# Attention of one hybrid layer: reciprocals by a small transposing transfer, both first scores ahead of the values, output weights loaded over a longer time

## The reference, cut to what matters

```python
s  = jnp.einsum('bqhd,bkhd->bhqk', qi, k).astype(jnp.float32) * ATTN_SCALE
pr = jax.nn.softmax(s, axis=-1).astype(v.dtype)
return jnp.einsum('bhqk,bkhd->bqhd', pr, v)
```

```python
mixed = jnp.concatenate([out_a, out_b, out_c], axis=-1)
return jnp.einsum('bnm,md->bnd', mixed, P['w_out'][l]), ckv, k_rope
```

## Time and profile before

| | |
|---|---|
| time, three runs | 1521.13, 1522.87 (median), 1523.97 us |
| profiled execution | 1522.13 us, its span 1520.2 us |
| granted TensorE clock | 0.997 of full speed |
| busy share of the span | PE 97%, PEld 78%, DVE 40%, ACT 27%, POOL 18% |
| attention, groups 0 to 3 | 273.5 to 352.9, to 430.5, to 508.2, to 608.1 us |

### The profile page before, as it was taken

The page is one execution under the profiler, slowest core; times in us unless marked ns, Lnnn a source line. Parts: engine busy times, 40 slices in busy tenths (PEclk is TensorE's granted clock), DMA queues, the critical chain, the costliest instruction groups (busy, mean ns, idle before and its releaser), DMA issues.

```text
span 1520.2 us, 25562 instructions
## 1 busy us (share of the span) xinstructions
PE 1480.5 (97%) x10145; PEld 1180.3 (78%) x10145; DVE 605.1 (40%) x1385; ACT 408.0 (27%) x933; POOL 280.3 (18%) x308
## 2 busy tenths in 40 slices
PE   6999999999999999999999999999999999999997
PEld 3654545666666655444899999999999999999996
DVE  2211446676868673136683222222222222222215
ACT  2400102555646452235321111111111111111114
POOL 0005400463747463110000100100000000000000
PEclk9999999999999999999999999999999999999999
DMA  9971001475747593541587999999889989899885
GB/s 364 353 261 50 32 0 41 82 137 104 142 98 144 130 200 73 194 166 70 191 322 271 323 294 312 315 353 300 291 316 296 362 293 300 313 292 357 291 260 223
DMA packets 313917, 338.79 MB, mean 223 GB/s; under 512 B 209091, under 2 KB 210666, under 8 KB 311678
## 3 DMA queue, kind: packets, MB, share of 16 engines
q1 hardware_dynamic: 308814, 319.58, 66.4%
q0 software_dynamic: 4752, 17.30, 4.4%
q10 hardware_dynamic: 288, 1.05, 0.2%
HBM read 266.18 MB, written 21.64 MB: 189 GB/s over the span
## 4 chain that ended last, share of the span: by engine, by line
PE 88%; DVE 5%; DMA 4%; ACT 2%; issue 1%; POOL 0%; SPq 0%; DVEq 0%; ACTq 0%; POOLq 0%
PE ps L1286 32%; PE ps L1315 16%; PE ps L678 8%; PE ps L1016 7%; PE ps L915 6%; PE ps L969 4%; DMA wreg<-wreg 2%; PE ps L703 2%; PE ps L869 2%; PE ps L693 1%; PE ps L894 1%; PE ps L881 1%; DVE stat L1921 1%; PE ps L710 1%; DMA wreg<-x_rows 1%
## 5 line engine op out<-in xcount | busy, mean ns | idle before, releaser
L1286 PE MATMUL ps<-mreg,wreg 128*128 128x144 f32 x4096 | 506.3, 286 | 0.0
L1286 PEld LDWEIGHTS ps<-mreg,wreg 128*128 128x128 f32 x4096 | 503.4, 190 | 0.7 <-ACT hreg L1625 0.4
L1315 PE MATMUL ps<-mreg,wreg 128*128 128x144 f32 x2048 | 256.4, 286 | 2.1 <-DVE mreg L2365 2.1
L1315 PEld LDWEIGHTS ps<-mreg,wreg 128*128 128x128 f32 x2048 | 253.1, 190 | 2.5 <-DVE mreg L2365 2.3
L2365 DVE TENSOR_TENSOR mreg<-ps,mreg 128x144 f32<-128x144 f32 x128 | 39.4, 307 | 357.6 <-PE ps L1286 346.7
L2530 POOL COPY wreg<-hreg 128x1024 uint16<-128x1024 uint16 x128 | 146.2, 1168 | 156.7 <-ACT hreg L1504 156.1
L915 PE MATMUL ps<-wreg 128*128 128x512 f32 (+2 forms) x400 | 159.0, 520 | 3.8 <-ACT hreg L1504 3.7
L1662 ACT ACTIVATE mreg<-ps 128x144 f32<-128x144 f32 x128 | 37.2, 291 | 426.1 <-PE ps L1286 426.1
L1016 PE MATMUL ps<-wreg,mreg 128*128 128x512 f32 x288 | 130.5, 598 | 0.0
L678 PE MATMUL ps<-hreg,wreg 128*128 128x512 f32 (+1 forms) x400 | 128.9, 480 | 0.0
L2577 POOL DMA_INDIRECT x_rows<-hreg,idx_s x15 | 23.9, 1596 | 533.1 <-DVE hreg L2342 521.6
(11 more groups left out here) (310 smaller groups left out, 1217.7 us busy)
## 6 DMA issues: line engine op xcount, KB each, us to landing
wreg<-in_w_e_dram SPq DMA_DIRECT2D x96, 2048.0 KB, 12.4
wreg<-in_w_ada_dram SPq DMA_DIRECT2D x16, 1024.0 KB, 8.3
wreg<-in_w_ada_dram SPq DMA_DIRECT2D x16, 512.0 KB, 10.9
wreg<-in_w_out_dram SPq DMA_DIRECT2D x8, 512.0 KB, 4.2
wreg<-in_x_sample_dram SPq DMA_DIRECT2D x8, 512.0 KB, 4.6
x_rows<-wreg SPq DMA_DIRECT2D x8, 512.0 KB, 3.5
xn_rows<-wreg SPq DMA_DIRECT2D x8, 512.0 KB, 2.6
wreg<-x_rows SPq DMA_DIRECT2D x8, 512.0 KB, 8.5
```

Source lines behind the costliest of these rows:

```text
L1286: mm = pe.matmul(o[:, 0:CAP], w[s][:, k, (f % 4) * P:(f % 4 + 1) * P], xsT[b][:, k, :], start=(k == 0), stop=(k == KD - 1))
L1315: mm = pe.matmul(bank[4 + dm % 2][:, 0:CAP], w2[f // 4][:, f % 4, dm * P:(dm + 1) * P], hidT[:, f, :], start=(f == 0), stop=(f == 7))
```

## The change: what it does

1. The reciprocals are turned by a transfer. POOL writes them, spread to 64 columns and split into 16-bit halves, into `rest_halves` (128 x 256 halves for a pair); SP issues one transposing transfer for the pair behind the four others (`turn_rest`), and ACT joins the halves into a part of `probT` (`rest_joined`). The 36 matmuls with the unit matrix and ACT's 36 copies out of their bank are gone. POOL waits for the small transfer of the pair before (`rest_turned`) before it writes the reciprocals of an even n. The constant `EXTRA` is 0, so that nothing else goes by this way.
2. In ACT's order the join of the reciprocals stands between the two exponentials of a pair, and not before the first.
3. At the start of a group PE makes the scores of n = 0 and n = 1 and then all values. ACT copies the values out instead of DVE.
4. Of the eight parts of the output weights two are loaded in group 1 and two in group 2 (behind n = 5 and n = 9), and four in group 3 (behind n = 2, 5, 8, 11).
5. `probT`, `w_rs` and the small buffers have other places in memory.

```diff
@@ sync
+                if n % 2:
+                    turn_rest(i, n // 2)
+
+            def turn_rest(i, t):
+                if t:
+                    turn_out(sp, i, t - 1, "rest")
+                sp.wait_ge(halves_split, prob_split(i, 2 * t + 1, 2))
+                sp.dma_start_transpose(out=rest_halves_T, in_=rest_halves).then_inc(rest_turned, 16)
+
+            def w_out_part(k):
+                sp.dma_start(w_out_sb[:, k, :], w_out[0, k * P:(k + 1) * P, :]).then_inc(side_in, 16)
...
                 for n in range(1, 16):
                     turn_prob(i, n)
+                    if i and n in (5, 9):
+                        w_out_part(2 + 2 * i + n // 9)
                 sp.wait_ge(s_mm, (i + 1) * 18)
                 move_queries(i + 1)
+                turn_rest(i, 8)
             sp.wait_ge(q_moved, 4 * 64)
             for n in range(16):
                 turn_prob(3, n)
-                if n < KD:
-                    sp.dma_start(w_out_sb[:, n, :], w_out[0, n * P:(n + 1) * P, :]).then_inc(w_out_in, 16)
+                if n % 3 == 2 and n < 12:
+                    w_out_part(n // 3)
...
+            turn_rest(3, 8)
@@ tensor
-                for ch in range(3):
-                    score(i, 0, ch)
-                values(i, 0)
-                values(i, 1)
-                for ch in range(3):
-                    score(i, 1, ch)
-                values(i, 2)
+                for n in range(2):
+                    for ch in range(3):
+                        score(i, n, ch)
+                for g in range(3):
+                    values(i, g)
...
-                    for t in range(NT):
-                        if REC_BESIDE[t] == (n, ch):
-                            pe.wait_ge(halves_split, prob_split(i, 2 * t + 1, 2))
-                            mm = pe.matmul(rec_at(t), rec_cols[t % 2], ident, start=True, stop=True)
                     mm.then_inc(t_mm, 1)
@@ scalar
+                def rest_joined(t):
+
+                    act.wait_ge(rest_turned, (i * NT + t + 1) * 16)
+                    act.activation(rest_of(t).bitcast(U16).rearrange("p (c h) -> p h c", h=2),
+                                   rest_halves_T.rearrange("p (h k) q -> p h (k q)", h=2), ACT.Copy).then_inc(t_out, 1)
...
                 exponential(0)
+                values_out(0)
+                values_out(1)
                 exponential(1)
+                values_out(2)
                 for n in range(2, 16, 2):
                     if n >= 4:
                         joined(n - 3, 0)
                     turned(n - 2, 2)
                     if n >= 4:
-                        rec_evict((n - 4) // 2)
                         exponential(n - 1)
+                        rest_joined((n - 4) // 2)
                     exponential(n)
                     turned(n - 1, 2)
@@ vector
+                highest(i, 1)
                 reciprocals(0)
-                highest(i, 1)
-                values_out(i, 2)
                 reciprocals(1)
@@ gpsimd
+                if i or t:
+                    pool.wait_ge(rest_turned, (i * NT + t) * 16)
+                rest = rest_halves.rearrange("p (h c) -> p h c", h=2)
...
                 pool.wait_ge(rec_ok, i * 18 + n + 1)
-                if t >= 2:
-                    turn_out(pool, i, t - 2, "rec")
-                pool.tensor_copy(rec_cols[t % 2][:, 64 * j:64 * j + 64],
-                                 a_rec[:, n % 4:n % 4 + 1].to_broadcast([P, 64])).then_inc(halves_split, 1)
+                at = 2 * EXTRA * P + 64 * j
+                pool.tensor_copy(rest[:, :, at:at + 64],
+                                 a_rec[:, n % 4:n % 4 + 1].bitcast(U16).unsqueeze(2).to_broadcast([P, 2, 64])
+                                 ).then_inc(halves_split, 1)
```

## The result

The change made the kernel slower: 1529.54 us median (1527.71 to 1531.67, six runs) against 1523.01 (1521.13 to 1524.46, six runs), a ratio of 1.0042 with a 95% interval of 1.0029 to 1.0055. 1516.2 was predicted, within 1511 to 1522. The profiled execution of the changed kernel took 1531.67 us, the longest of the six, its span 1529.9. That is 9.7 us above the span of before: 4.6 of them lie in group 0 (83.93 for 79.33 us), whose length also varies between runs for a cause that is open; groups 1 and 2 are 3.3 and 3.8 longer, and what follows is 2.2 shorter.

What follows compares the result with a forecast made beforehand. PE (7.49 us a pair) bounds groups 1 and 2, with ACT's ring (7.44) close behind; loads delay group 3. Terms 7.9 - 0.6 - 0.3 + 0.2 + 2.3 - 2.8 = 6.7 us off 1522.87 give 1516.2, range 1511 to 1522.

Steps and rivals of the forecast that it cites:

- The step that failed: Small transfer ahead of even n's in SP's queue: up to 1.0 us later, covered by DVE's idle time, cost 0.
- bounds of a price: POOL's copy of the reciprocals after the small transfer lands: 0.23 to 0.74 us, done before the next odd split.
- The loads: Output weights: four loads in groups 1 and 2 cost 2.8 us, group 3 gets 2.3 us back.
- the 0.3 us left: Slack between the odd exponential's end and PE asking for it, set against a load's 1.0 us later landing.
- a 4.5: Group 3's five pairs: 4.5 us lost, put down to loads between transposing transfers; half was to come back.
- The groups' ends: Last small transfer delays ACT's copy of the next keys: 0.1 us at each of three ends, 0.3 us lost.
- The reciprocal matmuls: 36 matmuls leave PE at 0.22 us each: 7.9 us won, range 4.3 to 7.9.
- The scores' order: Group starts, both first scores ahead of the values: 0, bounds 0 and 0.9 us four times.
- POOL's wait: POOL waits for the odd n's small transfer before writing an even n's reciprocals: 0.7 us left over, cost 0.
- C: Rival, 12%: small transfer becomes the ring through POOL, landing 3.3 us, pairs 7.8 us, time 1532 us.
- A: Rival, 18%: the four loads in groups 1 and 2 cost 1.7 us each instead of 0.7; time 1520 us.

Runs made afterwards that it cites:

- e10: Changed kernel with DVE's folds of the next heads' weights moved behind the join of the odd n; 1526.43 us, ratio 1.0023.
- e12: e10 plus a wait: POOL starts an even n's split only after DVE's second join of the even n before; 1526.13 us, ratio 1.0020.
- e1: Kernel before with only the output-weight loads changed: two each in groups 1 and 2, four in group 3; 1521.95 us, ratio 0.9987.
- e7: Kernel before with output-weight loads at the ends of groups 0 and 1 and ahead of group 3's first transfers; 1520.42 us, ratio 0.9978.
- e6: Changed kernel with ACT's join of a group's last small transfer behind its copies of the next keys; 1526.82 us, ratio 1.0020.
- e13: e11 with two buffers, the small transfer issued behind the next even n's transfers, and ACT's join of it behind the even exponential; 1516.61 us, ratio 0.9952.
- e14: e11 with POOL's split of an even n waiting for DVE's second join; 1516.65 us, ratio 0.9954.
- e2: Kernel before with only the scores' order changed, both first scores ahead of the values, which ACT copies; 1524.66 us, ratio 1.0006.
- e4: Changed kernel with two buffers for the small transfer, so POOL waits for the pair before the last; 1530.38 us, ratio 1.0052.
- e11: e10 with output-weight loads at the groups' ends and the group's last join behind the keys; 1518.16 us, ratio 0.9965.

## Why the prediction was wrong

**The step that failed** is "DVE joins these; it is busy 25.07 of 30 us, so 1.2 us of each pair are idle and cover that. Cost: 0". Idle time was counted, but not where it lies; the same step named the way out, "up to 1.0 us a pair if the idle time lies elsewhere", and the sum left it at nothing. The even n's transfers came 1.3 us later, and DVE's idle time for transfers rose by 14 us (25.6 to 39.9). They also moved DVE's work beside POOL's split: in the pair shown the second join took 1.58 for 0.85 and the fold 1.07 for 0.27, (1.58 - 0.85) + (1.07 - 0.27) = 1.5 us of 8.43, so an estimated 6.9 without. In the sum over the attention the folds paid for this (6.7 us for 2.4), the joins did not (88.8 for 88.9); e10, which moves the folds, gives back 1.1 and 1.5 us in groups 1 and 2, and e12, which parts the second join and the split, another 0.8 and 0.5 that the time does not show. The earlier trace rows held the warning: the same copy of reciprocals takes 0.74 and 0.23 us within one pair. The prediction took these as bounds of a price and did not ask what each ran beside.

**The loads** were the second part. 0.7 us a load was forecast for groups 1 and 2, and e1 gives 0.3 to 0.4; on top of the small transfer they cost (80.94 - 78.43)/2 = 1.3 and (81.49 - 78.23)/2 = 1.6. A price that rests on slack (the 0.3 us left) holds only as long as no other part of the same change takes that slack. Group 3 gave back 1.8 of the 2.3 forecast in e1. The 2.3 was half of a 4.5 that was put down to the loads whole; e7 shows 2.4 for the loads and 2.1 for DVE's routing tables.

**The groups' ends** were forecast at 0.1 us each and cost 0.4 and 0.5 in groups 1 and 2, which e6 gives back, since the last small transfer was reckoned from POOL's copy, without the four moves of queries that stand ahead of it on SP.

**What held.** The reciprocal matmuls are worth 0.22 us in a pair that nothing disturbs: these take 7.27 to 7.32 us in after, and e13 has three in a row in group 1. A whole group did not win the nine times 0.22 = 2.0: against e7, with the loads in the same place, e13's groups 1 and 2 are 0.5 and 0.9 us shorter, e14's 0.8 and 0.7. ACT's join takes 0.48 (0.3 to 0.5), the landing 2.4 (2.2), the issue 1.20 (1.0). The scores' order costs nothing (e2). That POOL's wait costs nothing held as a price (e4), though the wait itself was there 27 times, where 0.7 us was to be left over.

**The rivals.** C forecast 1532 us and a ring through POOL's wait; its time was close by luck, its cause was not there: e4 takes that wait away and nothing moves, and the small transfer lands after 2.4 us, not 3.3. A priced a load at 1.7 us: near what it costs with the small transfer, and far from the 0.3 to 0.4 without.

**What stays open**: why group 0 takes from 79.2 (e7) to 83.9 us (after); what keeps groups 1 and 2 of e11, e13 and e14 near 77 us, where 77.67 - 2.0 = 75.7 would do; and how much the place in the queue costs by itself, since no run moves it alone.

## What to carry to other kernels

Where an engine of an almost balanced pipeline does work that is late, look at what it will then run beside, on POOL and DVE above all, before its idle time is counted as cover, and sum the line over the whole stage before one pair is taken for the cause. When several parts of a change each live on the same slack, price them together. A small transfer costs an issue as long as that of a large one: put it where the queue's next entries are not on the ring, and look at everything that stands in that queue at a stage's end.

## What was not expected of the hardware

In after, a DVE copy of 1024 halves from SBUF to SBUF takes 0.72 to 0.76 us alone and up to 1.60 beside a POOL copy; a 128x128 product by a column 0.27 (in before and e13) and 1.07; POOL's copies 1.04 and 1.55, and 0.29 and 0.81. DVE's search for the highest, which reads PSUM, takes 1.47 to 1.49 us beside a POOL copy or not. A transposing transfer of 2 blocks lands in 2.4 us where 8 blocks take 3.1, but its issue occupies SP for 1.20 us, against 1.23.
